# The first product of a squared-ReLU MLP with weight blocks standing still and activations moving, in a two-block fp32 kernel

## What is computed

```python
D_MODEL, SEQ = 2048, 256
D_FF = 4 * D_MODEL
...
x = x + token_mixing(...)                      # second block, attention part
h = rmsnorm(x, norm_mlp)                       # x * rsqrt(mean(x*x) + eps) * gain
x = x + relu(h @ w_mlp_in) ** 2 @ w_mlp_out    # 2048 -> 8192 -> 2048
return rmsnorm(x, norm_final)
```

## Time and profile before

| | |
|---|---|
| median of 3 runs | 3095.2 us (3094.76 to 3096.69) |
| the profiled execution, its own time | 3095.27 us |
| its span | 3093.4 us |
| granted TensorE clock, mean | 0.999 |
| PE busy | 3059.5 us (99%) |
| PEld busy | 2591.0 us (84%) |
| DVE busy | 1777.1 us (57%) |
| ACT busy | 1460.8 us (47%) |

### The profile page before, as it was taken

How to read it: one execution, slowest core, us unless ns; L and a number is a source line. 1 busy time by engine, 2 the same in 40 slices (tenths; PEclk the granted TensorE clock), 3 DMA queues, 4 the chain that set the end, 5 groups by cost and what they waited for, 6 DMA issues and landing times.

```text
span 3093.4 us, 40246 instructions
## 1 busy us (share of the span) xinstructions
PE 3059.5 (99%) x14596; PEld 2591.0 (84%) x14596; DVE 1777.1 (57%) x2357; ACT 1460.8 (47%) x1797; POOL 636.5 (21%) x455
## 2 busy tenths in 40 slices
PE   8999999999999999999999999999999999999998
PEld 7999888888888888888888888899888888888886
DVE  5445564689854444565565556645776454545444
ACT  5445454555544444444444344554565534444353
POOL 3110000188888886000000000000000000000000
PEclk9999999999999999999999999999999999999999
DMA  6764467678887778777776675554446666666664
GB/s 209 244 209 139 146 216 252 191 217 218 217 221 217 214 218 263 259 238 238 238 234 214 223 251 183 188 183 149 134 138 192 189 191 190 190 190 186 193 184 149
DMA packets 215974, 627.58 MB, mean 203 GB/s; under 512 B 58139, under 2 KB 58789, under 8 KB 215472
## 3 DMA queue, kind: packets, MB, share of 16 engines
q1 hardware_dynamic: 156544, 549.79, 57.4%
q0 software_dynamic: 54464, 59.30, 7.7%
q10 hardware_dynamic: 4848, 16.94, 1.4%
HBM read 587.78 MB, written 38.14 MB: 202 GB/s over the span
## 4 chain that ended last, share of the span: by engine, by line
PE 96%; DVE 2%; ACT 1%; issue 0%; DMA 0%; ACTq 0%; DVEq 0%
PE ps L1634 22%; PE ps L1632 22%; PE ps L1633 22%; PE ps L1785 8%; PE ps L1787 8%; PE ps L1786 8%; PE ps L1893 1%; DVE w_lo L585 1%; PE ps L1734 1%; PE ps L1647 0%; PE ps L1753 0%; PE ps L1959 0%; PE ps L1698 0%; DVE big L1401 0%; PE ps L1879 0%
## 5 line engine op out<-in xcount | busy, mean ns | idle before, releaser
L585 DVE TENSOR_TENSOR w_lo<-raw,w_hi 128x1024 fp32r<-128x1024 f32 (+2 forms) x1072 | 1282.0, 1198 | 1158.3 <-ACT w_hi L580 1155.6
L580 ACT ACTIVATE w_hi<-raw 128x1024 fp32r<-128x1024 f32 (+2 forms) x1072 | 1106.7, 1034 | 1332.6 <-PE ps L1634 1021.1
L1632 PE MATMUL ps<-w_hi,a_hi 128*128 128x512 f32 x1536 | 602.2, 392 | 0.0
L1634 PE MATMUL ps<-w_hi,a_lo 128*128 128x512 f32 x1536 | 598.9, 390 | 0.0
L1633 PE MATMUL ps<-w_lo,a_hi 128*128 128x512 f32 x1536 | 598.5, 390 | 0.0
L1632 PE MATMUL ps<-w_hi,x_hi 128*128 128x512 f32 x1504 | 588.0, 391 | 0.0
L1634 PE MATMUL ps<-w_hi,x_lo 128*128 128x512 f32 x1504 | 586.2, 390 | 0.0
L1633 PE MATMUL ps<-w_lo,x_hi 128*128 128x512 f32 x1504 | 585.9, 390 | 0.0
L482 POOL DMA_INDIRECT gates<-srch x256 | 517.3, 2021 | 150.5 <-issue 75.9
L1785 PE MATMUL ps<-w_hi,x_hi 128*128 128x440 f32 (+2 forms) x1184 | 449.9, 380 | 4.0 <-DVE x_lo L1063 4.0
L1787 PE MATMUL ps<-w_hi,x_lo 128*128 128x440 f32 (+2 forms) x1184 | 437.9, 370 | 0.0
(11 more groups left out here) (324 smaller groups left out, 1657.5 us busy)
## 6 DMA issues: line engine op xcount, KB each, us to landing
raw<-in_peer_down SPq DMA_DIRECT2D x256, 512.0 KB
raw<-in_peer_up SPq DMA_DIRECT2D x256, 512.0 KB
raw<-in_w_mlp_in SPq DMA_DIRECT2D x128, 512.0 KB
raw<-in_w_mlp_out SPq DMA_DIRECT2D x128, 512.0 KB
raw<-in_w_in SPq DMA_DIRECT2D x112, 440.0 KB
raw<-in_w_in SPq DMA_DIRECT2D x96, 428.0 KB
raw<-in_w_out SPq DMA_DIRECT2D x64, 512.0 KB
gates<-zero POOLq DMA_DIRECT2D x32, 512.0 KB, 4.7
```

Source lines behind the costliest of these rows:

```text
L580: act.activation(w_hi[:, c % RING, 0:2 * n], raw[:, c % RING, 0:2 * n], ACT.Copy).then_inc(hi_made, 1)
L585: nc.vector.tensor_tensor(w_lo[:, c % RING, 0:2 * n], raw[:, c % RING, 0:2 * n], w_hi[:, c % RING, 0:2 * n].bitcast(F32), ALU.subtract).th ...
L1632: mm(o, xh, wh, start=(k == 0), stop=False)
L1634: last = mm(o, xl, wh, start=False, stop=(k == KT - 1))
```

## The change

- In the first product the weights now stand still: a 128x128 block of `w_hi` or `w_lo` is the stationary operand. Past a block of `w_hi` move 512 columns, the 256 tokens of `x_hi` and the 256 tokens of `x_lo` in one matmul (`x_hi` and `x_lo` are now halves of one tensor `x_hl`); past a block of `w_lo` move the 256 tokens of `x_hi`. The units come out on the partitions.
- A block fills four PSUM banks, one for each 128 units, with hi·hi + lo·hi in the first half of a bank and hi·lo in the second (`halves`). Blocks take banks 0 to 3 and 4 to 7 in turn.
- ACT copies the second halves to SBUF (`low_half`); DVE adds the first halves to them and does ReLU and square in one instruction; ACT makes `a_hi` and DVE `a_lo` from SBUF. The transposes, ACT's ReLU and its square are gone.
- The norm's factor, which ReLU let through and the square squared, is applied to the second product instead, as `rs_squared`, in the instruction that adds it to `h` (`add_scaled`).
- Block 0 of round 0 now waits for DVE's twelfth addition of "out2" (`d2 + 12`), and not the eleventh; the blocks of the second product use banks 0 to 7 in turn.

```diff
@@ act @@
                         for c in range(SUB):
+                            n = 4 * r + i - 1
                             if c == 3 and 1 <= i <= 4:
-
                                 act.wait_ge(chunk_used, SUB * B)
-                                before = h0 + 4 * r + i - 1
-                                if not static(before) or before > 0:
-                                    act.wait_ge(hid_turned, before)
-                                for t in range(NT):
-                                    last = act.activation(hid[:, t], ps[:, bank((i - 1) % 2, t), :], func, scale=rs(N_MLP, t))
-                                last.then_inc(copied_out, 1)
+                                act.wait_ge(copied_out, acts + n)
+                                act.activation(low_half, halves(i - 1)[:, :, 1], ACT.Copy).then_inc(low_copied, 1)
                             split_hi(act, B, c, WIDE)
-                            if c == 4 and 2 <= i <= 4:
-                                split_hidden(r, i - 2)
-                            if c == 7 and i == 4:
-                                split_hidden(r, 3)
...
+                            if c == 5 and 1 <= i <= 4:
+                                act.wait_ge(hid_full, h0 + n + 1)
+                                act.activation(a_hi[:, 4 * i - 4:4 * i, :], hidden, ACT.Copy).then_inc(hid_hi, 1)
@@ dve @@
+                def hide(r, i):
+                    n = 4 * r + i
+                    dve.wait_ge(low_copied, n + 1)
+                    V.tensor_tensor(hidden, halves(i)[:, :, 0], low_half, ALU.add).then_inc(copied_out, 1)
+                    dve.wait_ge(copied_out, sections[name][1] + n + 1)
+                    V.scalar_tensor_tensor(out=hidden, in0=hidden, scalar=0.0, in1=hidden, op0=ALU.max,
+                                           op1=ALU.mult).then_inc(hid_full, 1)
+
...
+                def add_scaled(B, pair, at):
+
+                    dve.wait_ge(chunk_used, SUB * (B + 1))
+                    for t in range(NT):
+                        to = h[:, t, at * WIDE:(at + 1) * WIDE]
+                        last = V.scalar_tensor_tensor(out=to, in0=ps[:, bank(pair, t), :], scalar=rs_squared[:, t:t + 1], in1=to,
+                                                      op0=ALU.mult, op1=ALU.add)
+                    last.then_inc(added_out, 1)
...
                         for c in range(SUB):
+                            if c == 3 and 1 <= i <= 4:
+                                hide(r, i - 1)
                             if c == 3 and (i >= 5 or (i == 0 and not first)):
-                                add_block(B - 1, (i - 1) % 2, (i - 5) % 4 if i else 3)
+                                add_scaled(B - 1, i - 5 if i else 3, i - 5 if i else 3)
                             split_lo(dve, B, c, WIDE)
-                            if c == 4 and 2 <= i <= 4:
-                                rest(r, i - 2)
-                            if c == 7 and i == 4:
-                                rest(r, 3)
+                            if c == 6 and 1 <= i <= 4:
+                                rest(r, i - 1)
@@ pe @@
+            def hidden_chunk(B, i, c):
+
+                pe.wait_ge(lo_made, SUB * B + c + 1)
+                for kk in range(2):
+                    k = 2 * c + kk
+                    both, xh = x_hl[:, :, k, :], x_hi[:, k, :]
+                    for jj in range(4):
+                        at = kk * WIDE + jj * P
+                        wh, wl = w_hi[:, c % RING, at:at + P], w_lo[:, c % RING, at:at + P]
+                        o = halves(i)[:, jj]
+                        if k == 0:
+                            mm(o, wh, both, start=True, stop=False)
+                            mm(o[:, 0], wl, xh, start=False, stop=False)
+                        else:
+                            mm(o[:, 0], wl, xh, start=False, stop=False)
+                            last = mm(o, wh, both, start=False, stop=(k == KT - 1))
+                last.then_inc(chunk_used, 1)
+
...
-                        if i < 2 and first:
-                            pe.wait_ge(copied_out, acts)
-                            pe.wait_ge(added_out, adds)
-                        elif 2 <= i < 6:
+                        if i == 0:
+                            pe.wait_ge(added_out, adds + 4 * r - 2)
+                        elif i == 1:
+                            pe.wait_ge(added_out, adds + 4 * r)
+                        elif i < 4:
                             pe.wait_ge(copied_out, acts + 4 * r + i - 1)
                         else:
-                            pe.wait_ge(added_out, adds + 4 * r + (i - 5 if i >= 6 else i - 1))
+                            pe.wait_ge(copied_out, acts + 4 * r + (3 if i < 6 else 4))
...
                     if c == 0:
-                        pe.wait_ge(added_out, d2 + 11)
+                        pe.wait_ge(added_out, d2 + 12)
                     pe.wait_ge(x_lo_made, 40 + c + 1)
-                    part(q2 + s, name, b, c, 0, WIDE, x_hi, x_lo, 0, 7)
+                    hidden_chunk(sections["mlp"][0], 0, c)
```

More of the change, by code:

```diff
@@ L185, in build @@
         rs34 = sb("rs34", [P, NT])
+        rs_squared = sb("rs_squared", [P, NT])
         gT = sb("gT", [P, 112])
@@ L214, in build @@
         hid_ring = big[:, 4096:8192].rearrange("p (i t n) -> p i t n", i=RING, t=NT)
+        low_half = big[:, 6144:7168].rearrange("p (j s) -> p j s", j=4)
+        hidden = big[:, 7168:8192].rearrange("p (j s) -> p j s", j=4)
         hid = big[:, 17184:18208].rearrange("p (t n) -> p t n", t=NT)
@@ L232, in build @@
         with ExitStack() as part:
-            x_hi = sb("x_hi", [P, KT, S], F32R, part)
-            x_lo = sb("x_lo", [P, KT, S], F32R, part)
+            x_hl = sb("x_hl", [P, 2, KT, S], F32R, part)
+            x_hi, x_lo = x_hl[:, 0], x_hl[:, 1]
             a_hi = sb("a_hi", [P, KT, S], F32R, part)
@@ L346, in build @@
         br_exp = sem("br_exp")
-        out_stored = sem("out_stored")
+        out_stored, low_copied = sem("out_stored"), sem("low_copied")
         sections = {}
@@ L379, in build, with halves @@
         out_and_sum = ps[:, 5, :].rearrange("p (j t b n) -> p j t b n", j=2, t=NT, b=2)
+        def halves(i):
+            at = 4 * (i % 2)
+            return ps[:, at:at + 4, :].rearrange("p j (h s) -> p j h s", h=2)
         def bank(parity, t):
@@ L596, in step, with rounds @@
                 act.wait_ge(act_step, steps[0])
-            def rounds(name, h0, count, func):
-                b0 = sections[name][0]
+            def rounds(name, h0, count):
+                b0, acts, _, _ = sections[name]
                 def one(r, first=0):
@@ L1003, in _ @@
                     root(N_MLP)
-            rounds("mlp", 4 * PEER_ROUNDS, MLP_ROUNDS, ACT.Relu)
+            rounds("mlp", 4 * PEER_ROUNDS, MLP_ROUNDS)
             for q in range(NQ):
@@ L1029, in rounds @@
                 b0 = sections[name][0]
+                def hide(r, i):
[5 more added lines that the diff above has]
+                                           op1=ALU.mult).then_inc(hid_full, 1)
                 def rest(r, i):
                     dve.wait_ge(hid_hi, h0 + 4 * r + i + 1)
-                    pair = ps[:, 4 + 2 * (i % 2):6 + 2 * (i % 2), :].rearrange("p b n -> p (b n)")
-                    V.tensor_tensor(a_lo[:, 4 * i:4 * i + 4, :].rearrange("p k s -> p (k s)"), pair,
-                                    a_hi[:, 4 * i:4 * i + 4, :].rearrange("p k s -> p (k s)").bitcast(F32),
+                    V.tensor_tensor(a_lo[:, 4 * i:4 * i + 4, :], hidden, a_hi[:, 4 * i:4 * i + 4, :].bitcast(F32),
                                     ALU.subtract).then_inc(hid_lo, 1)
+                def add_scaled(B, pair, at):
[5 more added lines that the diff above has]
+                    last.then_inc(added_out, 1)
                 def one(r, first):
@@ L1051, in rounds @@
                     one(r, False)
-                add_block(b0 + 8 * count - 1, 1, 3)
+                add_scaled(b0 + 8 * count - 1, 3, 3)
             def x_lo_tiles(j):
@@ L1605, in _ @@
                     inverse_root(N_MLP)
+                    dve.wait_ge(rs_made, N_MLP + 1)
+                    step(V.tensor_tensor(rs_squared[:], vrr[:, 2, N_MLP], vrr[:, 2, N_MLP], ALU.mult))
             rounds("mlp", 4 * PEER_ROUNDS, MLP_ROUNDS)
@@ L1637, in rounds @@
             def rounds(name, h0, count):
                 b0, acts, adds, _ = sections[name]
[L1640 to L1649, removed]
@@ L1665, in one @@
-                            chunk(b0 + 8 * r + i, i % 2, c, WIDE, x_hi if i < 4 else a_hi, x_lo if i < 4 else a_lo)
-                        if 1 <= i < 4:
-                            turn_hidden(r, i - 1)
+                            if i < 4:
+                                hidden_chunk(b0 + 8 * r + i, i, c)
+                            else:
+                                if i == 4 and c % 2 == 0:
+                                    pe.wait_ge(hid_lo, h0 + 4 * r + c // 2 + 1)
```

(1 more changed line is left out.)

8 lines of the change are left out of this document (removed).

## The result

The changed kernel takes **3143.3 us** (median of 5 runs, 3142.91 to 3144.28) against 3095.2 beside it: 1.0154 times, interval 1.0143 to 1.0165. It is 48 us slower, where I had forecast 3092.8, no change that three runs could tell, and a range up to 3107.

What follows compares the result with a forecast made beforehand. PE, busy 99% of the span, was taken to bound the kernel. Transposes -14.1, pairs +10.2 and seam +1.4 gave -2.5 us on 3095.27, so 3092.8 us, range 3083 to about 3107.

Steps and rivals of the forecast that it cites:

- the sum: Whole kernel: -14.1 us for transposes gone, +10.2 for first-product pairs, +1.4 for block 0's wait, together -2.5 us.
- my largest risk: First product: 512-column matmuls behind the short ones might not keep 226.8 ns; 10 ns there are 10 us.
- the transposes: MLP: 16 batches of 8 transposes on PE disappear, 0.88 us each, -14.1 us, with nothing hiding it.
- the pairs: First product: 1024 pairs of a 512- and a 256-column matmul, each replacing 340.2 ns of old cost; +10.2 us.
- the seam: Block 0 of the MLP: PE waits once for DVE's twelfth addition of "out2", +1.4 us, at most 1.6.
- The short matmul: First product: the 256-column matmul takes 123.4 ns, bounded by 111 and 135.3, against break-even at 113.4.
- rival 2: First product: the short matmul comes at its stream or load, 111 to 119.5 ns; kernel 3080.1 to 3088.8 us; chance 0.27.
- its sign, under 346, and mine, 350: First product's pair time in ns: under 346 means short matmul at stream or load; 350 means surcharge per instruction, chance 0.43.
- the shared bytes: First product: matmul and weight load share one flow of bytes, so 256 columns and a load take 135.3 ns; 3105 us.
- rival 3: First product: the weight load binds the pair, 132 ns and more; 3166 us if its recorded 190 ns counted; chance 0.25.
- DVE and ACT: MLP: ReLU and square about 1.4 us, DVE busy about 42 us longer, ACT shorter; all costed at 0.
- the slack: MLP rounds: 2.9 us between DVE's split of chunk 3 and PE's need of it, hiding DVE's added work.

Runs made afterwards that it cites:

- after_noshift: The changed kernel with rs_squared sharing the slot of rs34, so the activations keep the addresses of the kernel before: 3096.1 us, 0.9999 of the kernel before.
- after_moved: The changed kernel without the 32-byte shift, the MLP's hidden state in its own store 160 bytes modulo 256 from the weights: 3091.2 us, 0.9985 of the kernel before.

## Why the prediction was wrong

- **The step that failed** is the sum, "-14.1 + 10.2 + 1.4": it has no term for the 8,832 matmuls of 512 columns that the change doesn't edit, and so puts them at nothing without a reason. The reason that the prediction gives for the edited ones, "its operands are of the same type and its width is the same", fails for these. A matmul's price hung on something that neither type nor width shows, the distance between its operands in SBUF, and the addition of an 8-byte tensor changed that for every product in the kernel. What I had named as my largest risk, the 512-column matmuls behind the short ones, cost only 1.8 ns each. No rival had the unchanged ones.
- **What it measured.** 7,680 of them in the long sections went from 226.8 to 233.3, 49.9 us; 1,152 beside the attention from 227.8 to 233.1, 6 us. The 1,152 of 428 columns went from 195.3 to 193.5, -2 us. With the transposes -14.1, the pairs +7.2 (1024 x 7.0 ns), the seam +1.3 and the turns of the loop +0.8, the sum is 49.1; the measured difference is 48.1.
- **The transposes**: -14.1 stands, though no run takes it by itself. Their rows are gone, and the sum above leaves 1 us open. That of after_noshift (-14.1 + 1.3 + 1024 x 12.1 ns = 12.4, + 1.8 for its small waits) is 1.4 us; its profiled execution took 2.0 us more than that of the kernel before, its median 0.3 less. Its runs spread from 3093.5 to 3097.3, so a closer account isn't to be had from it.
- **The short matmul**: forecast 123.4 ns within 111 to 135.3, measured 118.6 in the changed kernel. The surcharge was mis-sized: 12 over the columns' 106.7 and not 16.7. It isn't one number, since it goes with the distance: at the distance of the kernel before, 256 columns behind 256 took 119.9, and elsewhere 113.6 to 120.2. 118.6 lies inside rival 2's 111 to 119.5, and the pair of 347 between its sign, under 346, and mine, 350, so neither is singled out. Neither the shared bytes of rival 3 (135.3) nor the recorded 190 ns of a load bound it.
- The Trainium skill's issue gap ("TensorE: Matmul & The Clock Gate") gives, as an estimate, 109.2 and 215.8 ns for 256 and 512 columns. No fp32r stream of these traces came to either: the best distances gave 113.6 and 226.6.
- **The seam**: forecast 1.4, measured 1.34. **DVE and ACT**: ReLU and square took 1.22 us and not 1.4, DVE was busy 37 us longer and not 42, and the slack held; I put nothing down for the turn of the loop over the rounds, whose branch held PE up twice, 0.8 us in all.
- **Without the shift** the forecast's terms nearly add up: after_noshift took 3096.1 and after_moved 3091.2, both inside the range, one on each side of 3092.8. In after_noshift the pair took 352 ns and not 350; that the totals agree doesn't prove each term.
- **Settled and open.** That the distance of the two SBUF operands sets the surcharge is shown in three ways: pads alone, a compensating pad, and a kernel of matmuls alone. What in the chip makes it so is not shown: a conflict between the reading of the moving operand and the load of the next weights would fit, since both run at the same time, but no run takes the loads away. Nor do I know why 440 columns don't mind, or why those of 428 became 1.8 ns faster with the shift.

## What to carry to other kernels

Where PE is never idle, compare the distance between two starts of an unchanged matmul before and after a change, first of all: here it told at once that the loss lay outside what had been edited. A tensor added in front of others moves them all; keep the large operands' addresses (an 8-byte tensor fits beside another one) or move both operands of a matmul together, and look at the distance modulo 256 bytes when fp32r streams of 512 columns matter. A change that swaps the operands' roles wants another distance than the old form, and can get it if one operand has a store of its own.

## What the runs showed of the hardware

- fp32r, 512 columns behind 512: 226.6 ns at the best distance of the operands and 234.3 at the worst, 3.4%, or 59 to 73 us in this kernel. It repeats with 256 bytes.
- fp32r, 256 columns: 113.6 to 120.2 ns; 440 columns: 200 at any distance, so 72 columns more cost 27 to 34 ns, depending on the distance.
- A weight load of 128 columns is recorded as 188 ns, and yet it hides behind a matmul of 256 columns: the next matmul, which needs that load, starts 118.6 ns after the short one.
- The branch of a loop on PE's sequencer took 0.21 us in the kernel before and 3.5 to 4.4 us in the changed one and its versions; in the changed one it cost PE 0.8 us for two turns, since the sequencer runs ahead.
